# Split weight tiles stored with the eight chunks of K side by side: the stationary operand is read at a step of 32 bytes

## The reference

```python
u = h @ P['ssd_w_in'][e]                                          # 1024 x 5664, layer 0
y = jnp.concatenate([y_a, y_b], axis=-1) @ P['mix0_w_out'][e]     # 2048 x 1024
q, k, v = split(h @ P['na_w_qkv'][o])                             # 1024 x 3072, layer 1
y = attn @ P['na_w_out'][o]                                       # 1024 x 1024
g = dwconv(h @ P['ffn_w_gate'][i], P['ffn_conv_w'][i])            # 1024 x 2816, both layers
ff = (gelu(g) * (h @ P['ffn_w_up'][i])) @ P['ffn_w_down'][i]      # 2816 x 1024, both layers
```

## Time and profile before

| | before |
|---|---|
| median of 3 runs | 1928.59 us (1928.18 to 1929.63) |
| profiled execution, first to last instruction (span) | 1928.4 us |
| PE busy | 1878.8 us, 97% |
| PEld (weight loads) busy | 1797.8 us, 93% |
| DVE / ACT / POOL busy | 1025.6 / 670.9 / 637.5 us |
| mean granted TensorE clock | 0.989 |

### The profile page before, as it was taken

How to read it: one execution, slowest core, us unless ns; L and a number is a source line. 1 busy time by engine, 2 the same in 40 slices (tenths; PEclk the granted TensorE clock), 3 DMA queues, 4 the chain that set the end, 5 groups by cost and what they waited for, 6 DMA issues and landing times.

```text
span 1928.4 us, 35126 instructions
## 1 busy us (share of the span) xinstructions
PE 1878.8 (97%) x13424; PEld 1797.8 (93%) x13424; DVE 1025.6 (53%) x1927; ACT 670.9 (35%) x1022; POOL 637.5 (33%) x309
## 2 busy tenths in 40 slices
PE   5999999999999999999999999999999999999997
PEld 3998888888899999999999999987899999999997
DVE  5747788877614655314554353557566553145543
ACT  4443333232413443312334321157444433123332
POOL 1223222222232323443335433433133234433341
PEclk9999999999999999999999999999999999999998
DMA  8334545445442222222222433211312222222122
GB/s 307 95 84 157 164 141 170 153 155 169 156 151 77 77 76 71 66 82 76 76 59 62 152 92 88 82 46 30 104 57 77 76 70 67 82 77 76 55 67 75
DMA packets 276232, 192.49 MB, mean 100 GB/s; under 512 B 25515, under 2 KB 259367, under 8 KB 275639
## 3 DMA queue, kind: packets, MB, share of 16 engines
q1 hardware_dynamic: 270982, 182.78, 31.1%
q10 hardware_dynamic: 5168, 8.58, 1.3%
HBM read 181.29 MB, written 10.04 MB: 99 GB/s over the span
## 4 chain that ended last, share of the span: by engine, by line
PE 89%; issue 5%; DVE 2%; ACT 2%; POOL 1%; DMA 1%; SPq 0%; POOLq 0%; ACTq 0%; DVEq 0%
PE ps L625 26%; PE ps L626 26%; PE ps L629 25%; PE ps L696 2%; POOL w_lo L560 1%; PE ps L1074 1%; PE ps L888 1%; PE ps L1054 1%; PE ps L1020 1%; DVE act_lo L1643 1%; ACT sp L1436 1%; PE ps L720 1%; PE ps L1093 0%; PE ps L873 0%; PE ps L808 0%
## 5 line engine op out<-in xcount | busy, mean ns | idle before, releaser
L560 POOL TENSOR_TENSOR w_lo<-raw,w_hi 128x1024 fp32r<-128x1024 f32 x244 | 601.4, 2467 | 1203.3 <-ACT w_hi L1127 1197.2
L625 PE MATMUL ps<-act_hi,w_hi 128*128 128x322 f32 x2752 | 847.5, 315 | 3.7 <-DVE act_lo L1643 2.2
L626 PE MATMUL ps<-act_lo,w_hi 128*128 128x322 f32 x2624 | 799.7, 312 | 0.0
L629 PE MATMUL ps<-act_hi,w_lo 128*128 128x322 f32 x2752 | 631.8, 311 | 0.0
L625 PEld LDWEIGHTS ps<-act_hi,w_hi 128*128 128x128 f32 x2752 | 522.0, 190 | 17.0 <-issue 13.7
L626 PEld LDWEIGHTS ps<-act_lo,w_hi 128*128 128x128 f32 x2624 | 497.7, 190 | 0.0
L629 PEld LDWEIGHTS ps<-act_hi,w_lo 128*128 128x128 f32 x2752 | 466.1, 189 | 0.0
L1127 ACT ACTIVATE w_hi<-raw 128x1024 fp32r<-128x1024 f32 x244 | 256.2, 1051 | 361.5 <-PE ps L629 321.9
L625 PE MATMUL ps<-f_hi,w_hi 128*128 128x322 f32 x704 | 213.6, 311 | 0.0
L626 PE MATMUL ps<-f_lo,w_hi 128*128 128x322 f32 x704 | 212.9, 310 | 0.0
L1958 DVE SCALAR_TENSOR_TENSOR x<-ps,mod,x 128x128 f32 (+1 forms) x96 | 48.4, 546 | 270.0 <-PE ps L629 269.4
(11 more groups left out here) (297 smaller groups left out, 1932.0 us busy)
## 6 DMA issues: line engine op xcount, KB each, us to landing
ada<-in_ada_w SPq DMA_DIRECT2D x40, 1024.0 KB, 6.1
raw<-in_ssd_w_in SPq DMA_DIRECT2D x44, 512.0 KB, 4.0
raw<-in_ffn_w_gate SPq DMA_DIRECT2D x44, 512.0 KB, 3.8
raw<-in_ffn_w_up SPq DMA_DIRECT2D x44, 512.0 KB, 3.8
raw<-in_ffn_w_down SPq DMA_DIRECT2D x32, 384.0 KB, 3.4
raw<-in_na_w_qkv SPq DMA_DIRECT2D x24, 512.0 KB, 3.8
raw<-in_ffn_w_down SPq DMA_DIRECT2D x32, 320.0 KB, 3.2
first<-in_ada_w SPq DMA_DIRECT2D x16, 512.0 KB, 10.2
```

The lines of the kernel that those rows point to most:

```text
L560: g.tensor_tensor(w_lo[:, s], raw[:, s % RAW], w_hi[:, s], ALU.subtract).then_inc(S["low_split"], 1)
L625: t.matmul(out, hi, chunk_of(src_hi, k0 + k, cols), start=start, stop=False)
L626: t.matmul(out, hi, chunk_of(src_lo, k0 + k, cols), start=False, stop=False)
L629: mm = t.matmul(half_out(2 * tset, h), lo, chunk_of(src_hi, k0 + k, cols), start=False, stop=stop)
```

## The change

The two rings `w_hi` and `w_lo` change their shape from [128, 4, 8 * 128] to [128, 4, 128, 8]: element (k, n) of a slot is now at n * 8 + k. For each column n the eight chunks of K stand side by side, 32 bytes in all. The bytes per slot, the number of slots and of instructions, their order on every engine, the semaphores and the DMAs stay as they are. `raw` keeps its layout.

Three kinds of instruction get other access patterns. PE's weight load for a chunk reads 128 columns with a step of 8 elements (32 bytes) where it read them with a step of 4 bytes. ACT's copy reads `raw` as before and writes `w_hi` with the step of 32 bytes, in 8 rows of 128. POOL's subtraction reads `raw` as before, reads `w_hi` and writes `w_lo` with the step of 32 bytes. The moving operands and PSUM are untouched.

```diff
-        w_hi = sb("w_hi", [P, RING, C * P], F32R)
+        w_hi = sb("w_hi", [P, RING, P, C], F32R)
...
-        w_lo = sb("w_lo", [P, RING, C * P], F32R)
+        w_lo = sb("w_lo", [P, RING, P, C], F32R)
...
-                g.tensor_tensor(w_lo[:, s], raw[:, s % RAW], w_hi[:, s], ALU.subtract).then_inc(S["low_split"], 1)
+                src = raw[:, s % RAW].rearrange("p (k n) -> p k n", k=C)
+                g.tensor_tensor(w_lo[:, s].rearrange("p n k -> p k n"), src, w_hi[:, s].rearrange("p n k -> p k n"), ALU.subtract).then_inc(S["low_split"], 1)
...
-                    hi, lo = w_hi[:, s, k * P:k * P + P], w_lo[:, s, k * P:k * P + P]
+                    hi, lo = w_hi[:, s, :, k], w_lo[:, s, :, k]
...
-                a(w_hi[:, s], raw[:, s % RAW], ACT.Copy).then_inc(S["high_split"], 1)
+                a(w_hi[:, s].rearrange("p n k -> p k n"), raw[:, s % RAW].rearrange("p (k n) -> p k n", k=C), ACT.Copy).then_inc(S["high_split"], 1)
```

## The result

| | before | after |
|---|---|---|
| median | 1929.11 us (4 runs, 1928.18 to 1930.66) | 2927.38 us (4 runs, 2925.47 to 2928.01) |
| ratio | | 1.5172, 95% interval 1.5153 to 1.519 |
| span of the profiled execution | 1928.4 us | 2925.6 us |
| mean granted clock | 0.989 | 0.993 |

The changed kernel is slower by 998 us. I had forecast 2659 us and a range of 1927 to 2830 us: the direction was right and the size too small.

What follows compares the result with a forecast made beforehand. PE bounds the kernel, its weight load close behind. 10752 loads x 69.5 ns = 747 us, less 20, plus 3.5 at the start, gives 730 us over 1928.4: about 2659 us, range 1927 to 2830 us.

Steps and rivals of the forecast that it cites:

- PE and its loads as the limit, 109 ns under 148.5: Split GEMM before: PE's time bounds it; a 109 ns weight load hides under each 148.5 ns product, 39.5 ns to spare.
- 0.31 ns a column are free: PE's weight load: it may become dearer by 0.31 ns a column (39.5 ns over 128 columns) at no cost in time.
- No other cost in the changed kernel: ACT's copy and POOL's subtraction: even doubled, to 2.1 and 4.9 us, hidden under 10.5 us slots, except at the start.
- The load at 218 ns: PE's stepped weight load: 109 + 109 = 218 ns, so 69.5 ns more for each of 10752 loads, 747 us; chance 0.47.
- A slot's period: Distance between POOL's steps in the ConvFFN: 7.13 us before, 10.5 us forecast; still 7.13 would mean a free load.
- The 20 us taken off: Taken off the 747 us: PE's idle time hiding some of the slower GEMM, together with loads not hidden even before.
- the 3.5 us added for the start: First two slots: one ACT copy and one POOL step with no slot before to hide behind, 1.05 + 2.4 us.
- The DVE row: Profile row of a short DVE step reading in 32-byte jumps: 3 to 11 ns more for 16 elements, 0.2 to 0.7 each.
- two turns (327 ns): Rival for PE's load: two turns more, 327 ns, about 3830 us; chance 0.08 for several turns or a lower clock.
- Second rival, free loads and dearer POOL: Load free, POOL's step 4.9 us, delaying five-chunk slots and the mixer stage: about 1955 us, range 1935 to 1975; chance 0.13.
- the 15 us for these slots: Five-chunk slots: two take 8.85 us on PE, POOL would need 9.8; 0.95 x 16 pairs = 15 us.
- The lower clock with several turns: PE, waiting for loads dearer by several turns, is granted the lower clock; 137 ns of streaming become 274; joint chance 0.08.

Runs made afterwards that it cites:

- The experiment at half the clock: The kernel before with weight loads at a step of 32 bytes and most products cut to 128 moving columns: 3014.39 us, mean clock 0.56.

## Why the prediction was right in direction and wrong in size

- **PE and its loads as the limit, 109 ns under 148.5**: right. The short products gave 112 ns in the GEMM itself.
- **0.31 ns a column are free**: right where it was tried. At 12 bytes the time grew by what 175 ns has over 148.5 (285 us by this sum, 289 measured), so the free part does end at 148.5 ns; at 8 bytes the load stayed hidden but for 11 us.
- **No other cost in the changed kernel**: right to within 5 us; ACT doubled as its upper bound said (2.17 us), POOL grew by a fifth, less than its bound, and both stayed hidden.
- **The load at 218 ns**: this is the step that failed. "Each column misses one turn of the load's own rhythm, 0.85 ns more" took the load's own beat for the unit in which a late column is paid. The experiment at half the clock shows that the stepped load doesn't go by that beat at all: it takes about 240 ns at either clock, and 1.89 ns a line where I had 1.70. A slot's period, the sign I had named, came at 11.6 us in place of 10.5. That is 242.5 - 218 = 24.5 ns a load, 10752 x 24.5 = 263 us of the 267 us missing (2925.6 - 2658.9). The 20 us taken off were wrong as well: PE's idle time fell from 50 to 44 us, so only 6 us were taken back. These 14 us, less the 8 us that 10752 x 94 ns has over the growth of PE's busy time and the 3.5 us added for the start, which no row shows by itself, make up the rest: 263 + 14 - 8 - 3.5 = 265.5 us.
- **The range**: it ended at 2830 us because its upper end was built from one turn plus 11 ns, not from an open price. The DVE row (3 to 11 ns for 16 elements) was no measure for PE: at 0.2 to 0.7 ns an element it stood below the 1.04 ns that PE really paid. A bound from another engine's short instruction bounded nothing, and the next case up, two turns (327 ns), left everything between 230 and 327 ns to nobody.
- **Second rival, free loads and dearer POOL**: the kernels with plain loads and stepped writes are that case, with POOL alone at 1951 us and with ACT as well at 1961, both inside the 1935 to 1975 given for it. The mechanism held only in part: POOL took 3.1 us and not 4.9, so that it stayed under a slot of five chunks (4.4 us) and the 15 us for these slots had no ground; DVE in the mixer stage was the path with POOL alone, and with both it was the wait for `ada`, which the rival did not have. That the times lie inside is partly luck.
- **The lower clock with several turns**: the mean clock stayed at 0.993. It was far lower only in the two runs with the moving columns cut (0.664 and 0.56); in all others it was 0.984 or more.

## What to carry to other kernels

Count the 16-byte lines that a stationary operand touches, not its columns: in float32 a load that takes one element from each line costs 1.84 to 1.89 ns a column against 0.85, and this kernel's products of 322 moving columns (148.5 ns) can't hide its 242.5 ns. If a layout has to interleave chunks, interleave two of float32, not eight: in this kernel loads of columns 8 bytes apart cost 0.6%, 16 bytes apart 48%. And when a hidden resource turns dearer, the price need not be a multiple of its present one, since it need not go by the engine's own beat; give the range an open upper end until a run at the new access pattern exists.

## What the runs showed of the hardware that I had not expected

- The plain load follows TensorE's granted clock (112 ns at 1.00, 213 ns at 0.50), the stepped one doesn't (242.5 ns at 1.00 with 322 columns, about 240 at 1.00 and at 0.50 with 128).
- Cutting the moving columns to 128 made the GEMM *slower*: with plain loads at full clock a product took 112 instead of 148.5 ns, but for most of the time the granted clock was 0.50 and a product took 213 ns, 2330 us in all against 1929.
- A step of 12 bytes, which mixes lines hit once and twice, costs by the number of lines (1.82 ns each), between the prices of 8 and 16 bytes.
- ACT's write gets dearer in the same place as PE's read, between 8 and 16 bytes, and there nearly doubles (1142 to 2065 ns).
- A longer step on one engine can shift others out of each other's way: with ACT's copy stepped, DVE's step L1860 in the mixer went from 477 to 348 ns, though it was not touched itself.
